# A hybrid pooling and spatial-gating layer on eight cores: where stored weight units, operand sums and the last row blocks sit in a planned schedule

## The reference

```python
proj = einsum('bsd,dc->bsc', x, w_in)                  # 1024 -> 1536
xp, zg = proj[..., :512], gelu(proj[..., 512:])
pooled = causal_multiscale_pool(xp)                    # trailing means over 2, 4, 8, 16, minus the token
pool_out = einsum('bsgc,gcd->bsgd', pooled, pool_w) * pool_scale
u, v = zg[..., :512], zg[..., 512:]
sgu_out = u * (tril(w_s) @ layer_norm(v) + b_s)        # in chunks of 128 rows, 4 heads
mix = concat([pool_out, sgu_out]) @ w_out              # 1024 -> 1024
h = layer_norm(alpha * x + mix)
y = layer_norm(alpha * h + (silu(h @ w_gate) * (h @ w_up)) @ w_down)   # inner width 2816
```

## Time and profile before

| what | us |
|---|---|
| median of 3 runs | 2246.17 |
| lowest and highest of the 3 | 2216.03, 2248.02 |
| the profiled execution, its own time | 2217.75 |
| span of its slowest core (core 2), first to last instruction | 2216.2 |
| spans of the eight cores | 2204.8 to 2216.2 |
| PE busy on core 2 | 2158.5 (97%) |
| DVE, ACT, POOL busy on core 2 | 1613.7, 979.4, 596.6 |

### The profile page before, as it was taken

How to read it: one execution, slowest core, us unless ns; L and a number is a source line. 1 busy time by engine, 2 the same in 40 slices (tenths; PEclk the granted TensorE clock), 3 DMA queues, 4 the chain that set the end, 5 groups by cost and what they waited for, 6 DMA issues and landing times.

```text
span 2216.2 us, 34816 instructions; the slowest of 8 cores (2204.8 to 2216.2 us)
## 1 busy us (share of the span) xinstructions
PE 2158.5 (97%) x10055; PEld 975.6 (44%) x10104; DVE 1613.7 (73%) x2661; ACT 979.4 (44%) x1569; POOL 596.6 (27%) x605
## 2 busy tenths in 40 slices
PE   7999999999799999999999999999999999999996
PEld 3444444444344444444444444444444444444443
DVE  4778787687678788688767767776866686687757
ACT  3456655576654144415423441553155145415521
POOL 4334424243111060033006001520431062024204
PEclk9999999999899999999999999999999999999999
DMA  9699999999789686569667846756665675467542
GB/s 176 145 258 238 249 260 225 242 268 275 243 181 247 193 219 188 172 188 221 218 193 209 255 176 179 264 196 173 205 243 186 174 260 196 161 191 268 195 150 93
DMA packets 192473, 463.82 MB, mean 209 GB/s; under 512 B 78880, under 2 KB 106144, under 8 KB 192288
## 3 DMA queue, kind: packets, MB, share of 16 engines
q1 hardware_dynamic: 153056, 383.47, 54.2%
q0 software_dynamic: 39232, 78.13, 18.5%
HBM read 379.37 MB, written 114.16 MB: 223 GB/s over the span
## 4 chain that ended last, share of the span: by engine, by line
PE 89%; DMA 5%; issue 2%; DVE 2%; POOL 1%; ACT 1%; DVEq 0%; POOLq 0%; ACTq 0%; SPq 0%
PE ps L940 46%; PE ps L1013 23%; PE ps L727 8%; PE ps L626 4%; PE ps L596 4%; PE ps L643 4%; DMA sb_wx<-w_gu 2%; DMA sb_xT<-xT 1%; DMA scr_gu<-sb_wr 1%; DMA scr_n<-sb_hop 1%; POOL sb_rst L565 1%; PE ps L686 1%; ACT sb_zr L1081 0%; POOL sb_zr L1083 0%; DVE sb_hop L451 0%
## 5 line engine op out<-in xcount | busy, mean ns | idle before, releaser
L940 PE MATMUL ps<-sb_hop,sb_wx 128*128 128x512 f16 x3500 | 789.1, 379 | 5.1 <-DVE sb_sl L925 3.4
L940 PEld LDWEIGHTS ps<-sb_hop,sb_wx 128*128 128x128 f16 x3500 | 340.0, 98 | 423.1 <-issue 18.9
L1013 PE MATMUL ps<-sb_wx,sb_aop 128*128 128x512 f16 x1764 | 395.1, 379 | 1.6 <-DVE sb_zr L1003 1.6
L940 PE MATMUL ps<-sb_hop,sb_wr 128*128 128x512 f16 x1428 | 339.4, 379 | 4.1 <-ACT sb_u L880 2.1
L565 POOL TENSOR_TENSOR sb_rst<-sb_rst,sb_nhalf 128x1 f32<-128x1 f32 (+1 forms) x96 | 102.6, 1071 | 861.3 <-DVE sb_rst L563 860.4
L880 ACT ACTIVATE sb_u<-ps 128x512 f32<-128x512 f32 x352 | 206.4, 595 | 200.9 <-PE ps L940 199.7
L925 DVE TENSOR_TENSOR sb_sl<-ps,sb_u 128x512 f32<-128x512 f32 x176 | 121.1, 688 | 212.8 <-PE ps L940 182.1
L1013 PEld LDWEIGHTS ps<-sb_wx,sb_aop 128*128 128x128 f16 x1764 | 172.0, 98 | 211.2 <-issue 4.9
L1081 ACT ACTIVATE sb_zr<-sb_zr,sb_rst 128x1024 f32<-128x1024 f32 x62 | 70.5, 1147 | 392.1 <-POOL sb_rst L565 379.6
L880 ACT ACTIVATE ps<-ps 128x512 f32<-128x512 f32 x240 | 139.0, 581 | 179.2 <-PE ps L940 120.1
L940 PEld LDWEIGHTS ps<-sb_hop,sb_wr 128*128 128x128 f16 x1428 | 138.3, 98 | 175.9 <-issue 12.2
(11 more groups left out here) (91 smaller groups left out, 2345.4 us busy)
## 6 DMA issues: line engine op xcount, KB each, us to landing
sb_wx<-scr_gu SPq DMA_DIRECT2D x100, 896.0 KB, 7.3
sb_wx<-scr_dn SPq DMA_DIRECT2D x63, 896.0 KB, 6.0
sb_wr<-scr_gu SPq DMA_DIRECT2D x40, 896.0 KB, 7.6
sb_hr<-x SPq DMA_DIRECT2D x64, 512.0 KB, 15.0
scr_z<-sb_hr SPq DMA_DIRECT2D x64, 512.0 KB, 12.7
sb_zr<-scr_z SPq DMA_DIRECT2D x64, 512.0 KB, 3.6
out<-sb_zr POOLq DMA_DIRECT2D x56, 512.0 KB, 8.8
sb_wr<-scr_dn SPq DMA_DIRECT2D x25, 896.0 KB, 5.8
```

The costliest lines, as they stand in the source:

```text
L940: i_ = e.matmul(ps[:, bk.home, :], lhsT=wv_(u["s"])[:, APOS[m], k * 128:(k + 1) * 128], rhs=hop[:, BPOS[m], k, :], start=(k == 0 and m in ...
L1013: i_ = e.matmul(ps[:, bks[b_].home, :], lhsT=aop[:, AP2[m], j, b_ * 128:(b_ + 1) * 128], rhs=wv_(s)[:, o, :], start=(m in (1, 7) and j == ...
```

## The change

Five edits, none of which changes what is computed.

1. `fetch_gu`: the units of j = 3 to 10 are stored two columns (four units) per tile, j = 9 and 10 in tile 0, 7 and 8 in tile 1, 5 and 6 in tile 2, 3 and 4 in tile 3. Before it was j = 7 to 10 in tile 0, none in tile 1, then the same.
2. `early`: the 17 units of the mixer stage are spread at equal distances of 38.2 positions from mixer 2 on (at most two in a mixer, then 38 apart).
3. The left operand of the projection: `STEPS[None]` makes the difference of the two pool groups first, which needs neither gating product, and two sub-tiles trade places (`OPOS`). In the last mixer the pool groups come one place later (after the u head of the same number, where they came before it).
4. `LAST` takes both pairs of a product next to each other; h's sums of tile 0 move behind most of the last projection (`pos`), and the first two of the four go to POOL.
5. The last row block of the last tile: the order 5, 3, 7, 4 in place of 5, 7, 3, 4, and its product 5 a little ahead.

```diff
+OPOS = {**APOS, 7: 5, 3: 4}
 STEPS = {True: ((0, 4, 2, ALU.add), (4, 1, 4, ALU.subtract), (3, 0, 1, ALU.subtract), (5, 6, 3, ALU.subtract)),
+         None: ((5, 1, 4, ALU.subtract), (0, 4, 2, ALU.add), (3, 0, 1, ALU.subtract), (4, 6, 3, ALU.subtract)),
-LAST = ((1, 0), (1, 1), (2, 0), (2, 1), (7, 0), (6, 0), (4, 0), (5, 0), (7, 1), (3, 0), (6, 1), (4, 1), (5, 1), (3, 1))
+LAST = ((1, 0), (1, 1), (2, 0), (2, 1), (7, 0), (7, 1), (6, 0), (6, 1), (4, 0), (5, 0), (4, 1), (5, 1), (3, 0), (3, 1))
...
-            for o, x, y, op in STEPS[left]:
-                P.add("dve", lambda e, o=o, x=x, y=y, op=op: e.tensor_tensor(out=v[:, o], in0=v[:, x], in1=v[:, y],
+            for i, (o, x, y, op) in enumerate(STEPS[left]):
+                eng = "pool" if also and i < 2 else "dve"
+                P.add(eng, lambda e, o=o, x=x, y=y, op=op: e.tensor_tensor(out=v[:, o], in0=v[:, x], in1=v[:, y],
...
-                q = base + (20 + g if m < NMT - 1 else 9 + 2 * g)
+                q = base + (20 + g if m < NMT - 1 else 11 + 2 * g)
...
-                four(lambda p: place(p)[0], lambda p: place(p)[1], True, base + 24.5)
+                four(lambda p: place(p)[0], lambda p: place(p)[1], None, base + 24.5)
...
-                    pl, nm = place(APOS[m])
+                    pl, nm = place(OPOS[m])
...
-                          alloc=[bk] if m in (1, 7) else (), after=[xload[g0], xload[g1]] if m == (2 if t == NT - 1 else 1) else ())
+                          alloc=[bk] if m in (1, 7) else (), after=[xload[g0], xload[g1]] if m == 1 and t < NT - 1 else ())
...
-                keep = T == (0 if j >= NP - 4 else 2 if j >= NP - 6 else 3)
+                keep = T == (NP - 1 - j) // 2
...
-            sums(v, [f"H{p}" for p in range(NS)], pos + 0.5, False, 4,
+            sums(v, [f"H{p}" for p in range(NS)], pos + 0.5 if T else STEP * NMT + 12, False, 4,
                  {p: [f"HS{i}" for i in range(6) if (2, 3, 6)[i % 3] == p] for p in (2, 3, 6)} if T == 0 else {})
...
-                    for n, m in enumerate((5, 7, 3, 4)):
-                        step(m, b, base + 3 + b, base + 3 + b + 0.25 * n)
+                    for n, m in enumerate((5, 7, 3, 4) if b < 3 else (5, 3, 7, 4)):
+                        q = base + 3 + b + 0.25 * n - 0.4 * (b == 3 and m == 5)
+                        step(m, b, base + 3 + b if m != 5 else q, q)
...
-            at.setdefault(FIRST + i * (NMT - 1 - FIRST) // len(early), []).append(u)
+            pos = (FIRST - 1) * STEP + i * (NMT - FIRST) * STEP / len(early)
+            at.setdefault(int(pos // STEP), []).append((u, pos % STEP))
...
-            for i, u in enumerate(at.get(m, ())):
-                prep(u, STEP * m + 12 * i, False, [f"{'VUP'[i]}{m % 2}"])
+            for u, d in at.get(m, ()):
+                prep(u, STEP * m + d, False, [f"{'V' if d < 10 else 'U' if d < 20 else 'P'}{m % 2}"])
```

More of the change, by code:

```diff
@@ L449, in sums @@
             n = 512 * wide
-            for o, x, y, op in STEPS[left]:
-                P.add("dve", lambda e, o=o, x=x, y=y, op=op: e.tensor_tensor(out=v[:, o], in0=v[:, x], in1=v[:, y],
-                                                                             op=op),
-                      c_dve(n, 2), pos, reads=[names[x], names[y]], writes=[names[o]] + also.get(o, []))
+            for i, (o, x, y, op) in enumerate(STEPS[left]):
+                eng = "pool" if also and i < 2 else "dve"
+                P.add(eng, lambda e, o=o, x=x, y=y, op=op: e.tensor_tensor(out=v[:, o], in0=v[:, x], in1=v[:, y],
+                                                                           op=op),
+                      c_pool(n) if eng == "pool" else c_dve(n, 2), pos, reads=[names[x], names[y]],
+                      writes=[names[o]] + also.get(o, []))
         Z = -100.0
@@ L1055, in down @@
                 for b in range(4):
-                    for n, m in enumerate((5, 7, 3, 4)):
-                        step(m, b, base + 3 + b, base + 3 + b + 0.25 * n)
+                    for n, m in enumerate((5, 7, 3, 4) if b < 3 else (5, 3, 7, 4)):
+                        q = base + 3 + b + 0.25 * n - 0.4 * (b == 3 and m == 5)
+                        step(m, b, base + 3 + b if m != 5 else q, q)
                         if m in (3, 4):
-                            norm2(T, b if m == 3 else 4 + b, base + 3 + b + 0.25 * n + 0.3)
+                            norm2(T, b if m == 3 else 4 + b, q + 0.3)
         def norm2(T, i, pos):
```

## The result

| | before | after |
|---|---|---|
| median of all executions of the comparison, us | 2248.02 (13) | 2238.55 (13) |
| lowest | 2211.38 | 2235.64 |
| ratio, 95% interval | | 1.0085, 1.0052 to 1.0118 |
| executions that by their time have no core with the stretch described below | 2211.38, 2216.03 | none |

The median fell by 9.5 us and lies inside the predicted range, but the ratio says 0.85% slower where 13 us faster was forecast. The two don't contradict each other: the ratio compares only the executions that are near the fastest of each kernel. Of the kernel before, only the two at 2211 and 2216 lie within 1.5% of its lowest time, and the changed kernel has none of their kind. The spans of the cores show why. (View of the cores, changed kernel, profiled execution, 2239.53 us.)

A forecast was written before the change was run, and what follows sets the result against it. PE, busy 97% of the span, was taken as the bound, so only its waits and low clock could be won. Minus 4, 7, 1 and 2 make 14, taken as 13 us: 2246.2 - 13 = 2233, range 2196 to 2242.

The forecast's parts named there:

- The 7 us of edits 3 and 4: Last projection, every core: DVE taken as the bound, PE's last product at 582 instead of 588.7; bounds 0 to 17 us.
- the scale: Whole execution: forecast placed at the shown median, 28.4 us above the profiled execution, 2246.2 - 13 = 2233.
- Edit 2, -5.3 on core 2, -4 on the last: Mixer stage: spread early units remove core 2's 3.6 us wait and 1.7 us low clock; about 4 us in the metric.
- the mixer wait: At 427.7 us PE waits 3.6 us, in full on cores 1, 2 and 4, behind POOL's 13.3 us before a weight load.
- The first sum: Last projection: the sum freeing product 7 comes first of four, so PE resumes at about 553 instead of 555.66.
- The hold by POOL: Last projection: POOL's two sums of about 4.5 us hold DVE's two-SBUF-input instructions, costing 3 us (nothing to 9).
- Edit 1, -1: FFN stores over four tiles: tile 0 gains 1.5 us (0 to 3.1), tile 1 loses 0.5 (0 to 4).
- Edit 5, -2: End of the last tile: last eviction no longer held 3.2 us by another row block; minus 2 us (0 to minus 3).
- The sum: Whole kernel: minus 4, 7, 1 and 2 make 14 us, taken as 13 because another core may be last.
- my rivals: Last projection gives nothing, 2240 (16%); runs without waits, 2223 (11%); slower through tile 1, 2247 to 2252 (5%).

The follow-up runs named there:

- f1: Changed kernel with edit 2 alone undone; cores without the stretch end at 2209.9 us on the mean, against 2212.6 for the kernel before.
- groups 1, 3 and 4: Three sets of experiments on one chip, each beside the kernel before, whose executions without the stretch had medians of 2216.1, 2215.3 and 2217.1 us.
- c2: Changed kernel without edits 1 and 5, all h sums on DVE, row statistics behind the first FFN column; cores without the stretch 2206.6 us, before 2212.6.
- c3: c2 with edit 1 added; ratios to the kernel before 0.9906, 0.9954 and 0.9912 in three groups.
- c1: Changed kernel without edits 1, 4 and 5, so edits 2 and 3 only; cores without the stretch 2203.8 us, before 2212.6.
- g3: Changed kernel with all h sums on DVE and h of tile 0 multiplied by zero; cores without the stretch 2203.3 us, before 2208.8.
- h1: Changed kernel with edit 2 undone, on the first chip; cores without the stretch 2208.3 us, before 2210.0.
- g1: The changed kernel as it is, run again beside the kernel before; cores without the stretch 2204.6 us, before 2208.8.
- g2: Changed kernel with all h sums on DVE; cores without the stretch 2201.3 us, before 2208.8.

## Why the prediction was wrong, point by point

Two steps of the prediction failed. The 7 us of edits 3 and 4 took DVE alone as what bounds the last projection, and left out the work of ACT that falls due behind it. And the scale took the gap of 28 us between the executions as something that a change leaves alone.

**Edit 2, -5.3 on core 2, -4 on the last: right mechanism, larger, and with a price.** The waits of 3.6 us are gone; between 61 and 541 us PE of core 2 doesn't wait for another engine. POOL still stands 7 us before weight loads, most of it for the matmul that paces them, and nothing urgent is behind. Alone it gives 6, since it also re-plans the last projection. What I did not see is that the mixer wait kept cores apart; that this is why the stretch comes more often is inferred, not shown.

**Edits 3 and 4, -7: the first step that failed.** The first sum moved as forecast (edit 3, about -2.5; 2.1 in the traces). For the rest I summed DVE's work and took DVE as the bound; the projection did shrink, to 572 where I said 582. But the statistics of its rows hang on DVE and end on ACT, whose list I had left out: with product 3 last for both pairs, six squares come due together, ahead of the first FFN copies. There 5.8 us are lost. And of the 11.4 us that the projection gained, 8.0 come with edit 2 alone (e4), so only 3.4 are left for edits 3 and 4 on top of it. Projection and first column together: -7.8 us with edit 2 alone, -9.9 with edit 3, -5.4 with edit 4 too. Instead of -7, edits 3 and 4 brought +2.4 on top of edit 2. Without edit 2 (f1) they bring -4.8, so the credit also depends on the order; I had added the edits up as if each worked alone. The hold by POOL was as forecast (4.14 us a sum where I had 4.5, L759 stretched by 1.7 us) and costs 1 to 3 us, where I had 3.

**Edit 1, -1:** measured -1.5 as the change stands, with a scatter of 0.8. **Edit 5, -2:** measured 0 on the means, +0.8 in the traces. I had noted that product 4 then follows product 7 in its bank, at 1 us; together with the wait behind it, it was 1.9.

**The sum.** Without the stretch, 4 to 5 us are left of 13: 4.2 and 5.2 on the mean of the cores, 2211.2 (one execution) against 2215.3 on whole executions. With it the changed kernel is 10 us faster (2236.8 against 2247.9, 2237.6 against 2247.6). Like against like the direction was right both times. Why the stretch costs a core 29 us in the changed kernel and 31 to 34 in the kernel before is open: no profile of the kernel before has it. That the median of 2238.55 fell into the range is luck in part: it compares executions with the stretch on both sides, of which the forecast knew nothing.

**The reading of the scale: the second step that failed,** and the one that the ratio shows. I had seen that the profiled execution stood 28.4 us below the median, wrote that nothing in its profile says why, and moved my number by it. I now read that gap as the stretch: three times of the kernel before, two modes 30 us apart. The core clocks of those executions are not on record, but in groups 1, 3 and 4 the kernel before takes 2215 to 2217 us without the stretch and 2247 to 2248 with it. The change moves single microseconds within a mode and several tenths of all core pairs from one mode to the other. None of my rivals had a change of the share in it.

## What to carry to other kernels

Times that fall into two groups with a fixed gap are two modes; before forecasting, find what separates them in the clock and span of each core, and ask whether the change moves the share. When work is moved out of one stage, list what falls due at its new place on every engine, and first on the one that looks idle. A gain ahead of a stage that is bound by its loads is kept only if the loads are lightened too, as c2 and c3 show. And where a planner re-plans everything, edits don't add up: test them together and one by one.

## What the runs showed of the hardware that was not expected

A pair of cores, (0,1), (2,3), (4,5) or (6,7), goes to clock 0.81 together and stays there for about 160 us (158 to 164 in all the profiles that have it). The starts seen are 578 to 597 us in most of them, 60 (f1, c1), 694 (c3), 787 (g3) and 1265 us (h1). Each lies where matmul load rises after a lighter phase, but most such places pass without it. In one group it came on 14% of the pairs (c3), 20% (before), 45% (g1) or 91% (g2), by the order of a few microseconds of work, and on the second chip almost never (6 of 223 pairs). With zero operands it did not come at the usual place. It costs a core of the changed kernel 29 us of 2205.
